# The Mamba mixer's input projection: a fourth z unit ahead of the first convolution group, step sizes a unit later

## The reference

```python
def mamba2_mixer(u, w_in, conv_w, conv_b, dt_bias, a_log, d_skip, norm_g, w_out, ssm0, conv0):
    z, xbc, dt_raw = jnp.split(u @ w_in, [D_INNER, D_INNER + CONV_DIM], axis=-1)
    xbc_full = jnp.concatenate([conv0.astype(xbc.dtype), xbc], axis=1)
    conv = conv_b + sum(xbc_full[:, k:k + t_len] * conv_w[k] for k in range(CONV_W))
    xbc_act = jax.nn.silu(conv)
    ...
    dt = jax.nn.softplus(dt_raw.astype(F32) + dt_bias.astype(F32))
    a = -jnp.exp(a_log.astype(F32))
    y, h_last = ssd_scan(xs, dt, a, bm, cm, ssm0)
    y = y + d_skip.astype(F32)[:, None] * xs.astype(F32)
    gated = y.reshape(bsz, t_len, D_INNER) * jax.nn.silu(z.astype(F32))
```

## Time and profile before

| what | value |
|---|---|
| median of 3 runs | 1206.47 us |
| lowest and highest | 1205.98, 1207.15 us |
| the profiled execution's own time | 1207.45 us |
| its span, first to last instruction | 1205.6 us |
| PE, DVE, ACT busy | 99%, 73%, 57% of the span |
| mean granted TensorE clock | 0.997 |
| stage `sin` on PE | about 207 to 418 us of the span |

### The profile page before, as it was taken

One profiled execution on the slowest core, in us unless ns is written; L12 is line 12 of the kernel. 1 busy time (PEld: TensorE's weight loads), 2 busy tenths in 40 slices (PEclk: granted clock), 3 DMA queues, 4 the chain that ended last, 5 costly groups with the idle time before them and its releaser, 6 DMA issues.

```text
span 1205.6 us, 26606 instructions
## 1 busy us (share of the span) xinstructions
PE 1192.7 (99%) x9814; PEld 1161.3 (96%) x9814; DVE 876.4 (73%) x1398; ACT 685.0 (57%) x1111; POOL 242.1 (20%) x351
## 2 busy tenths in 40 slices
PE   8999999999999999999999999999999999999998
PEld 8999999998988899999999999999998899999998
DVE  6766645999999868667745987887468767667448
ACT  6545435776686657555546765555367665454345
POOL 1100002422222101222344333232035310000001
PEclk8999999999999999999999999999999999999999
DMA  7765554654445365867886587657742256555552
GB/s 273 247 211 178 185 180 140 249 189 171 162 162 164 130 214 173 331 215 253 280 294 229 210 273 282 213 185 226 250 149 88 61 163 213 184 175 186 179 178 86
DMA packets 62144, 239.08 MB, mean 198 GB/s; under 512 B 7288, under 2 KB 8480, under 8 KB 57696
## 3 DMA queue, kind: packets, MB, share of 16 engines
q1 hardware_dynamic: 55728, 197.01, 49.3%
q0 software_dynamic: 6064, 40.66, 9.2%
q10 hardware_dynamic: 288, 0.54, 0.1%
HBM read 226.87 MB, written 13.39 MB: 199 GB/s over the span
## 4 chain that ended last, share of the span: by engine, by line
PE 94%; DVE 4%; ACT 1%; issue 1%; DMA 0%; SPq 0%; DVEq 0%; ACTq 0%
PE bank L476 29%; PE bank L477 29%; PE bank L478 28%; DVE wlo L1509 1%; PE bank L840 1%; PE bank L835 1%; PE bank L861 1%; DVE xl L1528 1%; PE bank L647 0%; PE bank L891 0%; ACT under L1427 0%; PE bank L809 0%; PE bank L821 0%; PE bank L822 0%; PE bank L849 0%
## 5 line engine op out<-in xcount | busy, mean ns | idle before, releaser
L1509 DVE TENSOR_TENSOR wlo<-raw,whi 128x1024 fp32r<-128x1024 f32 x367 | 457.7, 1251 | 236.8 <-ACT whi L1045 235.5
L476 PE MATMUL bank<-xh,whi 128*128 128x264 f32 x2008 | 577.1, 287 | 5.1 <-DVE wlo L1711 3.4
L477 PE MATMUL bank<-xl,whi 128*128 128x264 f32 x2008 | 570.3, 284 | 0.0
L478 PE MATMUL bank<-xh,wlo 128*128 128x264 f32 x2008 | 569.9, 284 | 0.0
L1045 ACT ACTIVATE whi<-raw 128x1024 fp32r<-128x1024 f32 x367 | 385.6, 1055 | 251.7 <-PE bank L478 241.1
L476 PEld LDWEIGHTS bank<-xh,whi 128*128 128x128 f32 x2008 | 379.4, 189 | 9.4 <-issue 5.8
L477 PEld LDWEIGHTS bank<-xl,whi 128*128 128x128 f32 x2008 | 379.7, 189 | 0.8
L478 PEld LDWEIGHTS bank<-xh,wlo 128*128 128x128 f32 x2008 | 377.8, 188 | 0.0
L476 PE MATMUL bank<-hh,whi 128*128 (+1 forms) x896 | 255.5, 285 | 0.3 <-ACT gu L1395 0.3
L478 PE MATMUL bank<-hh,wlo 128*128 (+1 forms) x896 | 255.1, 285 | 0.0
L477 PE MATMUL bank<-hl,whi 128*128 (+1 forms) x896 | 254.4, 284 | 0.0
(11 more groups left out here) (330 smaller groups left out, 1018.2 us busy)
## 6 DMA issues: line engine op xcount, KB each, us to landing
raw<-weights SPq DMA_DIRECT2D x367, 512.0 KB, 3.6
under<-ssm POOLq DMA_DIRECT2D x8, 1024.0 KB, 6.4
xact<-ssm POOLq DMA_DIRECT2D x8, 1024.0 KB, 6.7
out_ssm_s<-xact POOLq DMA_DIRECT2D x8, 1024.0 KB, 6.3
xact<-dtx_rows POOLq DMA_DIRECT2D x5, 1024.0 KB, 10.0
zs<-dtx_rows POOLq DMA_DIRECT2D x2, 1024.0 KB, 12.8
x<-xT SPq DMA_DIRECT2D x4, 264.0 KB, 6.3
xact<-stat_rows POOLq DMA_DIRECT2D x2, 528.0 KB, 6.1
```

Source lines behind the costliest of these rows:

```text
L476: pe.matmul(out, whi[:, w, c], rh, start=start, stop=False)
L477: pe.matmul(out, whi[:, w, c], rl, start=False, stop=False)
L478: return pe.matmul(out, wlo[:, w, c], rh, start=False, stop=stop)
L1509: dve.tensor_tensor(wlo[:, s, :], raw[:, s, :], whi[:, s, :].bitcast(F32), ALU.subtract).then_inc(lo_ready, 1)
```

## The change

`Z_FIRST` gets a fourth unit, and group 0 has one z unit behind it in place of two. So slot 4 is a z unit where a convolution stood, the four convolution units of group 0 come a slot later (5 to 8), and from slot 9 on the order of units is as before. The DVE series is spread over slots 2 to 4 where it was in 2 and 3. ACT's gathering moves from slot 4 to slot 5, and `whi` of unit 10 is made ahead of it. The turning on PE and the copies on DVE move a slot later by the new `TOKENS_AT`; the sums over tokens (`PRE_AT + 3`) stay in slot 10. The number of units, of transfers and of operations stays.

```diff
-Z_FIRST = [0, 1, 2]
-Z_AFTER = {0: [3, 4], 1: [5], 2: [6], 3: [7], 4: [8], 5: [9], 6: [10], 7: [11, 12, 13, 14, 15]}
+Z_FIRST = [0, 1, 2, 3]
+Z_AFTER = {0: [4], 1: [5], 2: [6], 3: [7], 4: [8], 5: [9], 6: [10], 7: [11, 12, 13, 14, 15]}
...
 PRE_AT = 7
+TOKENS_AT = 8
...
-                if s_ == PRE_AT:
+                if s_ == TOKENS_AT:
                     pre_tokens()
                 if s_ == PRE_AT + 3:
                     pre_sums()
...
-                if 1 < s_ < len(SIN) and s_ != 5:
+                if 1 < s_ < len(SIN) and s_ != 6:
                     ahead("sin", 0, s_)
-                if s_ == 4:
-                    ahead("sin", 0, 5)
+                if s_ == 5:
+                    ahead("sin", 0, 6)
                     gather_sizes()
...
-                if s_ == 4:
+                if s_ == 5:
                     gather_steps()
...
                 if s_ == 2:
-                    dt_series((15, 13, 11, 9))
+                    dt_series((15, 13, 11))
                 if s_ == 3:
-                    dt_series((7, 5, 3))
+                    dt_series((9, 7, 5))
+                if s_ == 4:
+                    dt_series((3,))
                     dt_end()
-                if s_ == PRE_AT + 1:
+                if s_ == TOKENS_AT + 1:
                     pre_tokens()
```

## The result

The changed kernel took 1211.62 us (median of 6 runs, 1208.50 to 1213.42) against 1206.43 us before (6 runs, 1205.70 to 1207.15). The ratio is 1.004, 95% interval 1.003 to 1.005: slower, by 5.2 us, which is clear of the noise though only 0.4%. The forecast was 1207.9 us with a range to 1210.8. The runs of the changed kernel scatter over 5 us, those of before over 1.5 to 2.6.

The account below looks back on a forecast made before the run. The prediction took VectorE, behind PE in slots 0 to 8 and full up to 244 us, as deciding when PE goes on. -1.43 us at unit 9 and +2.91 at the sums gave 1206.47 + 1.48 = 1207.9 us, range 1206.9 to 1210.8.

Parts of the forecast that it names:

- The order's term: VectorE's new order up to unit 11: -1.43 us at unit 9 and +2.91 at the sums, net +1.48 us.
- Unit 9: On PE, waits for VectorE's take of unit 7; was to start at 231.56 us, 1.43 earlier than 232.99.
- wait 2.9 us at the sums: PE ahead of the sums over tokens, ready at 237.6 us, was to idle until VectorE's copies ended, about 240.5.
- The copies: VectorE's copies of the turned step sizes, needed by the sums, were to end at 240.46 us, 1.48 later than before.
- The take of unit 10: On VectorE behind the copies; claimed to stay at 241.2 us.
- ScalarE's rounding ahead of the gathering: `whi` of unit 10, 1.07 us on ScalarE, claimed hidden behind VectorE's series, with 0.4 us to spare.
- A: Forecast case: clock stays up, +1.5 us (0.7 to 1.9), 1207.9 us; chance 0.60.
- B: Slower rival: clock falls in PE's new gap at the sums; 1210.7 us, at most 1211.1; chance 0.28.
- B's price: PE at half clock some 6.0 us behind the gap at the sums: 2.7 us lost, up to 3.1.
- VectorE's idle time ahead of the take of unit 11: VectorE was to idle 1.7 us there, where it idled 0.28, as PE ends unit 11 1.48 us later.
- A with most given back: Lower end of the forecast range, 1206.9 us: clock up, most of the added wait recovered.
- The rival C: Faster rival: PE doesn't wait at the sums, unit 11 starts at 239.8 us; kernel 1205.1 us; chance 0.09.

Follow-up runs that it names:

- fill21: Changed kernel with 21 unread matmuls of 264 columns ahead of the sums over tokens on TensorE; 1208.29 us against 1206.06 before the change.
- after_look_a: Changed kernel run again unchanged, one traced execution; 1212.32 us against 1206.09 before the change.
- copies_1_later: Kernel before the change with only VectorE's copies of the turned step sizes one slot later; 1209.69 us against 1205.88.
- fill10: Changed kernel with 10 unread matmuls of 264 columns ahead of the sums over tokens; 1210.15 us against 1206.06 before the change.
- gap_then_dense: Kernel before the change with VectorE's copies one slot later and 24 unread 264-column matmuls between the wait and the sums; 1210.51 us against 1206.09.
- after_again: Changed kernel run again unchanged in a second set, 5 runs; 1209.22 us against 1206.06 before the change.
- copies_2_later: Kernel before the change with only VectorE's copies of the turned step sizes two slots later; 1212.74 us against 1205.88.
- sums_later: Changed kernel with the sums over tokens, ScalarE's copy and VectorE's reading of them moved from slot 10 to 11; 1206.06 us against 1206.06.

## Why the prediction was wrong, point by point

**The order's term was right.** Unit 9 was to come 1.43 us earlier, and the take that it waits for came 1.43 earlier. PE was to wait 2.9 us at the sums: 2.92. The copies were to end 1.48 us later: PE stood at the sums 1.50 later. The take of unit 10 was to stay: +0.03. ScalarE's rounding ahead of the gathering was hidden: it ended 0.1 us behind the series, and VectorE has no idle time before its take of unit 11. Net +1.48 was forecast, and +1.53 measured at the first chunk with the clock up (fill21). Nothing of it was given back.

**The step that failed is the choice between A and B.** The prediction put 0.60 on A, the clock stays up, and 0.28 on B, so its sum has nothing for the clock. B held in every one of four traces of the changed kernel, and none of its 13 runs was below 1208.5. The prediction itself named the question, whether a gap of 2.9 us counts as the one of 3.36 does, and said that its rows, 1.47 us without a fall and 3.36 us with one, don't tell. It does: in after_look_a the clock fell 0.9 us before the gap ended, as it did inside the gap at the start. The comparison by length also left something out. copies_1_later and fill10 fell behind gaps of 1.45 and 1.72 us, gap_then_dense did not behind 1.44: in front of unit 9 the wide matmuls resume at once, at the sums 2.2 us of narrow ones follow, which the earlier trace rows show. The row of 1.47 us without a fall was thus a poor witness for A. That a gap of half the length was enough at the sums is known only from kernels run later; with one row on each side, even chances were the most that A could claim.

**B's price was too low at its upper end, too.** It was taken from the start of the kernel: 2.7 us for one fall, at most 3.1. The traces have 1.52 us for 3.4 us at half clock (44.68 - 43.16), 3.08 for 6.8 and 4.21 for 10.2, of which 0.9 lie in the gap, where they cost nothing. 0.45 us for each us at half clock, from the start's 0.22 against 0.121, is right: 0.45 x 3.4 = 1.5. The estimate by the page "TensorE: Matmul & The Clock Gate" of the Trainium skill had 0.5 for each us, and 1211.0 in all; the traces have 0.45 (1.52 / 3.4). But the length of such a stretch was read off a single one of 6.8 us. The median of the first set, 5.19 - 1.53 = 3.7 us for the clock, lies between the second and the third; that of after_again, 3.16 - 1.53 = 1.6, is at the first. With B's stretch at 10 us, worth 4.2, the range would have reached 1212.2 and held the time. VectorE's idle time ahead of the take of unit 11, 3.29 us for 1.7, is the same term: PE did unit 11 at half clock. The range's lower end, 1206.9, is called A with most given back, but A's +0.7 gives 1207.2; nothing hangs on it.

**The rival C fell,** and for the reason given there: VectorE has no idle time in that stretch.

What stays open: why the stretch at half clock is short in one run and long in the next, and what it was in the two slowest runs of the first set, of which there is no trace. Most of all, no run tells whether the changed kernel would keep its clock if wide matmuls stood behind its gap of 2.9 us.

## What to carry to other kernels

When two engines are level, moving work ahead of a step that the other engine waits for only moves the wait, and here to a place where it costs more. Read a gap on TensorE together with what stands right behind it: a gap of some 1.5 us was free of a clock fall in front of wide matmuls and cost 1.5 to 3 us more in front of narrow ones, while one of 2.9 us brought the clock down in one trace before anything followed it. And where several kernels with different orders reach the same time, the amount of work is the bound, so take work off the engine, on to one that doesn't slow it.

## What the runs showed of the hardware

- The granted clock fell at gaps of 1.45, 1.72, 2.9 and 3.06 us in front of matmuls of 32 to 256 columns, in all seven traces that have one. In after_look_a (2.88 us) and copies_2_later (3.06 us) it fell before the gap ended, in the other five 1.0 to 2.6 us behind its end. It did not fall at 1.44 and 1.47 us in front of matmuls of 264 columns, nor at 0.38 us in front of the narrow ones. At half clock it stayed for 3.4, 6.8 or 10.2 us, in five of the seven traces with TensorE working all the time.
- The changed kernel's 13 runs span 1208.50 to 1213.42 us, sums_later's 11 runs 1204.71 to 1206.93; in the traces the length of the stretch at half clock accounts for 2.7 us of it (44.68 to 47.37). Such a stretch doesn't always bring scatter: copies_2_later's five runs span 1.5 us.
- The profile's clock column can miss half clock at a kernel's start: it reads 1.00 while matmuls start 0.22 us apart and not 0.12 (copies_1_later, 9 to 10 us).
- Two operations of GpSimd, 1.51 us, and the copy behind them slowed VectorE by 0.66 us, most of the 0.83 us that they saved it; four copies out of PSUM on ScalarE, 0.6 us, ran beside two operations of VectorE that took 0.87 us where they take 0.83.
